# Low rank products on another bank ring, key norms inverted as columns, and a weight load issued later, in the RWKV-7 heads of a hybrid block

## The chip, the cores and the metric

The kernel runs on one core of one Trainium2 chip. The metric is the time of one execution on the device in microseconds (us), lower is better. Everything is float32.

## The reference, cut to what matters

The program is a two layer block (RWKV-7 time mixing, then Hyena, each followed by a mixture of experts). The change lies in the features of the RWKV-7 mixer, which are made for 512 tokens (256 of context, 256 latent) and 16 heads of 64:

```python
wlog = -softplus(-(w0 + tanh(xw @ w1) @ w2)) - 0.5      # one w for each direction z
decay = exp(-exp(wlog))
a = sigmoid(a0 + (xa @ a1) @ a2)                        # one a for each direction z
k = xk @ wrkv[1]
kk = heads(k * k_k)
kk = kk / maximum(norm(kk, axis=-1), 1e-12)
k_dir = k * (1.0 + (a - 1.0) * k_a)
```

After that comes a scan over the tokens in both directions, S = S * w + (S kk) b + v k, with b = kk * a, from which the output rows are read.

## The kernel before, in words

`rwkv_heads` treats two heads (128 channels on the 128 partitions) at a time, in `CH` = 8 groups. The scan is done in chunks of 64 tokens: each group has 8 chain steps (`STEPS`), and each step has three phases, so a round has 24 slots (`SLOTS`). Round m (from -2 to 8) does the chain of group m (`chain`), the matrices of group m + 1 (`now`), and the features of group q = m + 2 (`early`); rows of group m - 1 (`behind`) are finished on the side. Rounds -2 and -1 have no chain yet, rounds 0 to 5 have all of it, round 6 has no `early` part, round 7 has only the chain. Every engine walks the same list of slots in program order: nothing is reordered, so an instruction that waits holds all behind it on its engine.

In each round, TensorE does in phase 0 `chain_state` (products with the state H; VectorE then makes G), in phase 1 `chain_solve` (with G; ScalarE then copies U), in phase 2 `chain_close` (with U; VectorE then makes the new H). Between these stand the other products.

PSUM banks are handed out by two written orders. `OPEN` uses banks 0 and 1 in turn, `INVERSE` banks 2, 3 and 4 in turn; a use may start when the use two (or three) places before it in the order has been read by its reader, ScalarE or VectorE (`BankUses.before`). In `OPEN` the part of slots 14 to 23 reads: wyc(n), h3(m), w0(q), w1(q), k(q), h4(m), a0(q), a1(q), norm(q), h5(m), rg(q). Here h0 to h5 are the six parts of `modulate` (a matrix product with `ada_w` for later layers, summed by VectorE), w and a the low rank products (`low_rank`, L776), k the key projection (`project`, L785), norm the sums of squares, rg the receptance and the gate. So w1 waits until VectorE has read h3 (`modulate(m, 3)`, slot 14, L1493).

The key norms: ScalarE squares k into `kk` (`keys`, L1103) and copies k to `kT` (L1104); TensorE multiplies the 128x512 squares by `head_ones` (L797), which gives each channel the sum of its head; ScalarE takes the root of 128x512 (`norm`, L1107, with a table load); VectorE takes the maximum with 1e-12 (L1298), inverts in two halves of 128x256 (L1301), and multiplies (`unit_keys`, L1305).

The weights of the next group are loaded by SyncE in `load_first` (six transfers, L305 to L310: w2, a2, two blocks of `rw_wrkv` of 512 KB, two parts of g2), in slot 4 of its own list; its semaphore `kr_in` is waited for by the first product of w. SyncE also issues `later.load` (L244, four pieces of `ada_w`) in slots 0, 3, 8, 12, 15 and 19, each after the product before has been done.

Of the kernel before, what the change touches and what calls it, by code (L numbers as in the profile page):

```python
# [17 lines left out]
ALU = mybir.AluOpType  # L18
# [509 lines left out]
def open_order():  # L528

    order = []  # L530
    for m in range(-2, CH + 1):
        chain, now, early, behind = 0 <= m < CH, 0 <= m + 1 < CH, m + 2 < CH, m >= 1
        order += [(m, u) for u in ("bl", "kl") if chain]
        order += [(m, u) for u in ("vl",) if chain]
        order += [(m - 1, u) for u in ("ys",) if behind]
        order += [(m, u) for u in ("h0", "wy0", "wy1") if chain]
        order += [(m, u) for u in ("h1",) if chain]
        order += [(m + 1, u) for u in ("v",) if now]
        order += [(m, u) for u in ("h2",) if chain]
        order += [(m + 1, u) for u in ("bc", "kc", "vc") if now]  # L540
        order += [(m - 1, u) for u in ("rows",) if behind]
        order += [(m + 1, u) for u in ("wyc",) if now]
        order += [(m, u) for u in ("h3",) if chain]
        order += [(m + 2, u) for u in ("w0", "w1", "k") if early]
        order += [(m, u) for u in ("h4",) if chain]
        order += [(m + 2, u) for u in ("a0", "a1") if early]
        order += [(m + 2, u) for u in ("norm",) if early]
        order += [(m, u) for u in ("h5",) if chain]
        order += [(m + 2, u) for u in ("rg",) if early]
    return order  # L550


def inverse_order():

    order = []
    for m in range(-1, CH):
        chain, now = m >= 0, m + 1 < CH
        order += [(m, u) for u in ("z1l", "s1l", "s2l") if chain]
        order += [(m + 1, u) for u in ("pc0", "pc1") if now]
        order += [(m, u) for u in ("z2l",) if chain]  # L560
        order += [(m + 1, u) for u in ("pl00", "pl01", "pl10", "pl11") if now]
        order += [(m, u) for u in ("xl",) if chain]
        order += [(m + 1, u) for u in ("z1c", "s1c", "s2c", "z2c", "xc") if now]
    return order
# [25 lines left out]

OPEN = BankUses(open_order(), 0, 2, lambda name: name == "ys" or name[0] == "h")
INVERSE = BankUses(inverse_order(), 2, 3, lambda name: name[0] in "zp")


def rwkv_heads(s, r, experts, ins, mods):
# [31 lines left out]
    wide = S1b  # L627
    spare = s.take(1)
    later = LaterModulation(s, ins, mods)
# [4 lines left out]
    names = ("ka_ready", "open_done", "open_act", "open_dve", "inv_done", "inv_act", "inv_dve",  # L634
             "sq_ready", "dec_ready", "ex_ready", "bon_ready", "feat_ready", "mask_ready",
             "m_ready", "sel_ready", "turned_in", "base_ready", "spread_ready", "turned_out", "start_ready",
             "h_ready", "g_done", "gs_ready", "u_done", "us_ready", "hy_done", "y_done", "y_ready",
             "y_var", "y_root", "yn_ready", "o_done")
    (ka_ready, open_done, open_act, open_dve, inv_done, inv_act, inv_dve,
     sq_ready, dec_ready, ex_ready, bon_ready, feat_ready, mask_ready,  # L640
     m_ready, sel_ready, turned_in, base_ready, spread_ready, turned_out, start_ready,
# [5 lines left out]
    def rows(n):  # L647
        return slice(n * C, (n + 1) * C)
# [52 lines left out]
    with nc.Block(name="rwkv_heads", no_gpsimd_drain=True) as block:  # L701

        @block.sync
        def _(sp):
            wo_rows = ins["rw_wo"][0].rearrange("(m p) n -> p m n", p=P)

            for m in ROUNDS[:-1]:
# [3 lines left out]
                for slot in range(SLOTS):  # L711
                    if slot == 4 and 0 <= n and n + 1 < CH:
                        sp.wait_ge(open_done, OPEN.done(n, "rg"))
                        r.load_first(sp, ins, n + 1)
# [42 lines left out]
        def _(pe):  # L757
# [12 lines left out]
            def low_rank(n, name):  # L770
                if name == "w":
                    pe.wait_ge(kr_in, 96 * (n + 1))
                w, x = (w2, r.wl) if name == "w" else (a2, r.al)
                banks = [open_bank(n, f"{name}{z}") for z in range(2)]
                for z in range(2):
                    pe.matmul(banks[z][:, :], w[rows(z), :], x[rows(z), :], start=True, stop=True).then_inc(open_done, 1)  # L776

# [17 lines left out]
            def norm(n):  # L795
                pe.wait_ge(sq_ready, n + 1)
                pe.matmul(open_bank(n, "norm")[:, :], s.c("head_ones"), kk, start=True, stop=True).then_inc(open_done, 1)  # L797

# [193 lines left out]
            for m in ROUNDS:  # L992
                n, q = m + 1, m + 2
                chain, now, early, behind = 0 <= m < CH, 0 <= n < CH, q < CH, m >= 1
                for slot in range(SLOTS):
# [37 lines left out]
                    if behind and slot == 13:  # L1033
                        out_rows(m - 1)
                    if now and slot == 14:
                        from_values_early(n)
                    if chain and slot == 14:
                        modulate(m, 3)
                    if early and slot == 14:
                        low_rank(q, "w")  # L1040
                    if early and 15 <= slot < 18:
# [5 lines left out]
                    if early and slot == 18:  # L1047
                        low_rank(q, "a")
                    if early and slot == 19:
                        norm(q)  # L1050
                    if now and slot == 20:
                        level_one(n, 0)
                    if chain and slot == 21:
                        modulate(m, 5)
# [23 lines left out]
        def _(act):  # L1078
# [13 lines left out]
            def decay_rank(n, z):  # L1092
                if n and z == 0:
                    act.wait_ge(feat_ready, n)
                act.activation(sg[z], read(n, f"w{z}")[:, :], ACT.Sigmoid, bias=vec(z, n)).then_inc(open_act, 1)  # L1095

            def rate_rank(n, z):
                bank = read(n, f"a{z}")
                act.activation(steps(BB[n % 2], z), chunks(bank[:, :]), ACT.Sigmoid, bias=vec(2 + z, n)).then_inc(open_act, 1)

# [5 lines left out]
            def norm(n):  # L1106
                act.activation(kk, read(n, "norm")[:, :], ACT.Sqrt).then_inc(open_act, 1)  # L1107

# [93 lines left out]
            for m in ROUNDS:  # L1202
                n, q = m + 1, m + 2
                chain, now, early, behind = 0 <= m < CH, 0 <= n < CH, q < CH, m >= 1
                for slot in range(SLOTS):
# [32 lines left out]
                    if behind and slot == 13:  # L1238
                        act.activation(outT, read(m - 1, "rows")[:, :], ACT.Copy).then_inc(open_act, 1)
                    if now and slot == 14:  # L1240
                        from_values_early(n)
                        spread(n)
                    if early and slot == 14:
                        decay_rank(q, 0)
                        decay_rank(q, 1)
                    if now and slot == 16:
                        place(n, 0)
                    if now and slot == 17:
                        place(n, 1)
                    if early and slot == 18:  # L1250
                        keys(q)
                        rate_rank(q, 0)
                        rate_rank(q, 1)
                    if early and slot == 19:
                        norm(q)
# [13 lines left out]
        def _(dve):  # L1269
            def decay_sum(n, z):  # L1270
                dve.wait_ge(open_act, OPEN.taken(n, f"w{z}")[1])
                for f in range(2):
# [21 lines left out]

            def key_norms(n, f):
                if f == 0:
                    dve.wait_ge(open_act, OPEN.taken(n, "norm")[1])
                    dve.tensor_scalar(kk, kk, 1e-12, None, ALU.max)  # L1298
                    dve.drain()
                c = slice(f * L, (f + 1) * L)  # L1300
                dve.reciprocal(kk[:, c], kk[:, c])  # L1301
                dve.drain()

            def unit_keys(n):
                dve.scalar_tensor_tensor(kk, kT, vec(4, n), kk, ALU.mult, ALU.mult)  # L1305
                dve.drain()

            def key_rates(n):
                dve.wait_ge(open_act, OPEN.taken(n, "a1")[1])
                if n >= 2:  # L1310
# [236 lines left out]
            for m in ROUNDS:  # L1547
                n, q = m + 1, m + 2
                chain, now, early, behind = 0 <= m < CH, 0 <= n < CH, q < CH, m >= 1
                for slot in range(SLOTS):  # L1550
# [37 lines left out]
                    if chain and slot == 11:  # L1588
                        modulate(m, 2)
                    if now and slot == 12:  # L1590
                        base_level(4, wide)
                        bonus(n)
                    if now and slot == 13:
# [31 lines left out]
                    if early and slot == 23:  # L1625
                        unit_keys(q)
                        rates(q)
# [1205 lines left out]
```

## Time and profile before

| what | value |
|---|---|
| median of 3 runs | 1949.21 us (1948.52 to 1949.31) |
| profiled execution, its own time | 1943.13 us |
| its span, first to last instruction | 1941.3 us |
| TensorE matmuls busy | 1727.5 us (89%) |
| VectorE busy | 769.4 us (40%) |
| ScalarE busy | 513.6 us (26%) |
| GpSimd busy | 52.9 us (3%) |
| mean DMA rate | 260 GB/s |

The profiled execution has 1.8 us outside its span. The heads stage lies between about 70 us and 700 us of the span; after it come stages of expert weights. Times in the rows are in us from the start of the span, and an engine's share of busy time is a mean over stages with different limits.

### The profile page before, as it was taken

How to read it: one execution, taken by the hardware profiler on the slowest of the kernel's cores; microseconds unless marked ns; L12 is line 12 of the kernel's file. 1: busy time of each engine (PE TensorE's matmuls, PEld its weight loads, DVE VectorE, ACT ScalarE, POOL GpSimd, SP SyncE). 2: the span in 40 equal slices, each digit the busy share in tenths (PEclk: the TensorE clock that was granted, in tenths of full speed). 3: DMA queues.
4: the chain of work that ended last, by engine and by line, in shares of the span. 5: the costliest groups of instructions: out<-in, count | busy, mean ns of one | idle time of the engine just before them, and what ended most of it. 6: DMA issues, size and time to landing. Idle time of an engine off the chain costs nothing. (4 is left out here: it accounts for less than half of the span.)

```text
span 1941.3 us, 36382 instructions
## 1 busy us (share of the span) xinstructions
PE 1727.5 (89%) x15051; PEld 943.6 (49%) x15051; DVE 769.4 (40%) x1926; ACT 513.6 (26%) x969; POOL 52.9 (3%) x45
## 2 busy tenths in 40 slices
PE   5777887887887888999999999898899999999996
PEld 2345655655655554443443443675654444444442
DVE  5667777776776335210100101565836110110111
ACT  3244454453453121111111111313221111111111
POOL 0001100100100000000000001000000000000001
PEclk8979999998998989999999999999989999999999
DMA  9013323323334477999999997233167999999993
GB/s 311 14 46 100 107 82 117 104 83 110 105 105 137 144 301 311 428 428 429 428 429 428 428 417 278 81 129 124 75 271 300 426 428 429 428 429 429 427 419 123
DMA packets 105463, 504.17 MB, mean 260 GB/s; under 512 B 15840, under 2 KB 60656, under 8 KB 79472
## 3 DMA queue, kind: packets, MB, share of 16 engines
q1 hardware_dynamic: 104064, 501.93, 65.2%
q8 instruction: 99, 1.62, 0.4%
q10 hardware_dynamic: 1264, 0.33, 0.1%
q14 instruction: 36, 0.29, 0.0%
HBM read 501.13 MB, written 1.09 MB: 259 GB/s over the span
## 5 line engine op out<-in xcount | busy, mean ns | idle before, releaser
L2016 DVE TENSOR_TENSOR arena<-banks,arena 128x512 f32<-128x512 f32 x32 | 22.1, 692 | 659.3 <-PE banks L1828 659.3
L1828 PE MATMUL banks<-arena 128*64 128x512 f32 x1024 | 226.2, 594 | 9.5 <-DMA arena<-in_moe_w_up 9.5
L1850 PE MATMUL banks<-arena 128*64 128x512 f32 x1024 | 226.8, 595 | 3.3 <-ACT arena L1947 3.3
L1819 PE MATMUL banks<-arena 128*64 128x512 f32 x1024 | 225.3, 592 | 3.3 <-DVE arena L1939 3.3
L785 PE MATMUL banks<-arena 128*128 128x512 f32 (+1 forms) x384 | 166.0, 571 | 3.2 <-ACT arena L1095 3.0
L1828 PEld LDWEIGHTS banks<-arena 128*64 128x64 f32 x1024 | 81.4, 137 | 152.3 <-issue 152.2
L1819 PEld LDWEIGHTS banks<-arena 128*64 128x64 f32 x1024 | 74.3, 137 | 147.8 <-issue 144.2
L1850 PEld LDWEIGHTS banks<-arena 128*64 128x64 f32 x1024 | 70.7, 137 | 154.5 <-issue 150.7
L1941 ACT ACTIVATE arena<-banks,arena 128x128 f32<-128x128 f32 x128 | 48.2, 457 | 334.1 <-PE banks L1808 334.1
L1808 PEld LDWEIGHTS banks<-arena 128*128 128x128 f32 x1024 | 118.3, 194 | 28.1 <-issue 24.3
L1808 PE MATMUL banks<-arena 128*128 128x128 f32 x1024 | 124.4, 280 | 3.5 <-DVE arena L2011 3.5
L1857 PE MATMUL banks<-arena 128*128 128x512 f32 x256 | 115.4, 593 | 2.4 <-ACT arena L1952 2.4
L785 PEld LDWEIGHTS banks<-arena 128*128 128x128 f32 x384 | 72.1, 201 | 60.8 <-issue 46.8
L1951 ACT ACTIVATE arena<-banks 128x512 f32<-128x512 f32 x32 | 19.1, 597 | 282.5 <-PE banks L1850 282.5
L2435 PE MATMUL banks<-arena 128*128 128x256 f32 x384 | 87.5, 386 | 0.0
L1939 DVE TENSOR_SCALAR arena<-banks,arena 128x128 f32<-128x128 f32 x128 | 43.7, 404 | 96.9 <-PE banks L1808 96.9
L2435 PEld LDWEIGHTS banks<-arena 128*128 128x128 f32 x384 | 73.4, 193 | 16.7 <-issue 6.6
L1857 PEld LDWEIGHTS banks<-arena 128*128 128x128 f32 x256 | 46.1, 190 | 50.0 <-issue 45.9
L1932 ACT ACTIVATE arena<-banks 128x512 f32<-128x512 f32 x32 | 19.1, 597 | 169.7 <-PE banks L1819 169.7
L253 PE MATMUL banks<-arena 128*32 128x96 f32 (+1 forms) x1536 | 48.1, 265 | 9.0 <-DMA arena<-in_ada_w 5.3
L776 PE MATMUL banks<-arena 64*128 64x512 f32 x64 | 22.2, 768 | 28.6 <-DVE arena L1493 20.3
L1475 DVE SCALAR_TENSOR_TENSOR arena<-banks,arena 128x64 f32<-128x64 f32 x112 | 26.8, 280 | 50.5 <-PE banks L967 47.3
(401 smaller groups left out, 2433.3 us busy)
## 6 DMA issues: line engine op xcount, KB each, us to landing
arena<-in_moe_w_gate SPq DMA_DIRECT2D x64, 2048.0 KB, 14.9
arena<-in_moe_w_up SPq DMA_DIRECT2D x64, 2048.0 KB, 17.1
arena<-in_moe_w_down SPq DMA_DIRECT2D x64, 2048.0 KB, 13.3
arena<-in_ada_w SPq DMA_DIRECT2D x128, 192.0 KB, 2.9
arena<-in_ada_w SPq DMA_DIRECT2D x64, 256.0 KB, 3.6
arena<-in_rw_wrkv SPq DMA_DIRECT2D x24, 512.0 KB, 5.1
arena<-in_hy_w_in SPq DMA_DIRECT2D x6, 2048.0 KB, 8.6
arena<-in_ada_w SPq DMA_DIRECT2D x8, 1024.0 KB, 16.8
```

What stands on the lines that cost most here:

```text
L253: mm = pe.matmul(bank[g * 32:(g + 1) * 32, 0:n], self.cond[:, half * self.HALF + t], self.w[t][:, g * n:(g + 1) * n], start=(t == 0), stop ...
L776: pe.matmul(banks[z][:, :], w[rows(z), :], x[rows(z), :], start=True, stop=True).then_inc(open_done, 1)
L785: mm = pe.matmul(s.psum[OPEN.bank(n, name)][:, 0:width], wkv[k][:, t], x[:, t], start=(t == 0), stop=(t == KT - 1))
L1475: dve.scalar_tensor_tensor(H[:, z], s.psum[5 + z][:, 2 * C:3 * C], fade[m % 2][:, z, j:j + 1], Hf[:, z], ALU.mult, ALU.add)
L1808: mm = pe.matmul((X0, X1)[k // 4][:, k % 4 * P:(k % 4 + 1) * P], hx[:, t, k * P:(k + 1) * P], sel[par][:, t].rearrange("p a b -> p (a b)") ...
L1819: mm = pe.matmul(G[j * CAP:(j + 1) * CAP, :], xT[:, t, j * CAP:(j + 1) * CAP], wg[par][j][:, t], start=(t == 0), stop=(t == KT - 1))
L1828: mm = pe.matmul(U[j * CAP:(j + 1) * CAP, :], xT[:, t, j * CAP:(j + 1) * CAP], wu[j][:, t], start=(t == 0), stop=(t == KT - 1))
L1850: mm = pe.matmul(bank[j * CAP:(j + 1) * CAP, :], hT[:, t, j * CAP:(j + 1) * CAP], wd[j][:, t, half * 512:(half + 1) * 512], start=(t == 0) ...
L1857: pe.matmul(OUT[k][:, :], selwT[par][:, k // 2], y[:, k % 2 * 512:(k % 2 + 1) * 512], start=start, stop=stop).then_inc(scat_done, 1)
L1939: op = eng.tensor_scalar(xT[:, k], src, sc[:, k:k + 1], sh[:, k:k + 1], ALU.mult, ALU.add)
L1941: op = eng.activation(xT[:, k], src, ACT.Identity, bias=sh[:, k:k + 1], scale=sc[:, k:k + 1])
L2435: mm = pe.matmul(s.psum[n % 2][:, 0:L], win_ring[k][:, t, q * P:(q + 1) * P], hT[:, t], start=(t == 0), stop=(t == KT - 1))
```

## The change

There are four edits.

1. The low rank products w0, w1, a0, a1 leave `OPEN` and take banks of `INVERSE`, between xl(m) and z1c(m + 1). TensorE issues w in slot 13 instead of 14 and a in slot 14 instead of 18; ScalarE reads w in slot 13 instead of 14, and a in slot 17 instead of 18.
2. The key norms are made as 128x8: TensorE uses a block of 128 tokens of the squares as the stationary operand and two columns of `head_ones` as the moving one, four times, so the sums stand with tokens on the partitions. ScalarE takes the root of 128x8, VectorE the maximum and the inverse of 128x8, and TensorE spreads them back to 128x512 with eight products of a broadcast column with the identity (`spread_norms`, a new use "inv" of `OPEN`, slot 20), which VectorE reads from PSUM in `unit_keys` (slot 21 instead of 23). TensorE's norm moves from slot 19 to 18. A root of one element at the end of slot 17 draws the table load ahead.
3. `load_first` is issued in slot 9 instead of 4.
4. On VectorE `modulate(m, 0)` moves from slot 3 to 2 and `bonus` from slot 12 to 11.

```diff
@@ open_order
-        order += [(m + 2, u) for u in ("w0", "w1", "k") if early]
+        order += [(m + 2, u) for u in ("k",) if early]
         order += [(m, u) for u in ("h4",) if chain]
-        order += [(m + 2, u) for u in ("a0", "a1") if early]
-        order += [(m + 2, u) for u in ("norm",) if early]
+        order += [(m + 2, u) for u in ("norm", "inv") if early]
@@ inverse_order
-    for m in range(-1, CH):
-        chain, now = m >= 0, m + 1 < CH
+    for m in range(-2, CH):
+        chain, now, early = m >= 0, 0 <= m + 1 < CH, m + 2 < CH
...
         order += [(m, u) for u in ("xl",) if chain]
+        order += [(m + 2, u) for u in ("w0", "w1", "a0", "a1") if early]
         order += [(m + 1, u) for u in ("z1c", "s1c", "s2c", "z2c", "xc") if now]
@@ SyncE
-                    if slot == 4 and 0 <= n and n + 1 < CH:
+                    if slot == 9 and 0 <= n and n + 1 < CH:
                         sp.wait_ge(open_done, OPEN.done(n, "rg"))
                         r.load_first(sp, ins, n + 1)
@@ TensorE
-                banks = [open_bank(n, f"{name}{z}") for z in range(2)]
+                banks = [inverse_bank(n, f"{name}{z}") for z in range(2)]
...
             def norm(n):
                 pe.wait_ge(sq_ready, n + 1)
-                pe.matmul(open_bank(n, "norm")[:, :], s.c("head_ones"), kk, start=True, stop=True).then_inc(open_done, 1)
+                bank = open_bank(n, "norm")
+                for t in range(TOK // P):
+                    mm = pe.matmul(bank[:, 2 * t:2 * t + 2], kk[:, t * P:(t + 1) * P], s.c("head_ones")[:, 0:P:HEAD], start=True, stop=True)
+                mm.then_inc(open_done, 1)
+
+            def spread_norms(n):
+                bank = open_bank(n, "inv")
+                pe.wait_ge(inv_norms, n + 1)
+                for t in range(TOK // P):
+                    for h in range(2):
+                        one = norms[:, 2 * t + h:2 * t + h + 1].to_broadcast([P, HEAD])
+                        mm = pe.matmul(bank[rows(h), t * P:(t + 1) * P], one, s.c("ident"), start=True, stop=True)
+                mm.then_inc(open_done, 1)
...
+                    if early and slot == 13:
+                        low_rank(q, "w")
...
                     if early and slot == 14:
-                        low_rank(q, "w")
+                        low_rank(q, "a")
...
                     if early and slot == 18:
-                        low_rank(q, "a")
-                    if early and slot == 19:
                         norm(q)
...
+                    if early and slot == 20:
+                        spread_norms(q)
@@ ScalarE
-                act.activation(kk, read(n, "norm")[:, :], ACT.Sqrt).then_inc(open_act, 1)
+                act.activation(norms, read(n, "norm")[:, 0:2 * TOK // P], ACT.Sqrt).then_inc(open_act, 1)
...
+                    if early and slot == 13:
+                        decay_rank(q, 0)
+                        decay_rank(q, 1)
...
+                    if early and slot == 17:
+                        rate_rank(q, 0)
+                        rate_rank(q, 1)
+                        act.activation(spare, s.c("ones")[:, 0:1], ACT.Sqrt)
                     if early and slot == 18:
                         keys(q)
-                        rate_rank(q, 0)
-                        rate_rank(q, 1)
-                    if early and slot == 19:
                         norm(q)
@@ VectorE
-                c = slice(f * L, (f + 1) * L)
-                dve.reciprocal(kk[:, c], kk[:, c])
-                dve.drain()
+            def key_norms(n):
+                dve.wait_ge(open_act, OPEN.taken(n, "norm")[1])
+                dve.tensor_scalar(norms, norms, 1e-12, None, ALU.max)
+                dve.drain()
+                dve.reciprocal(norms, norms).then_inc(inv_norms, 1)
             def unit_keys(n):
-                dve.scalar_tensor_tensor(kk, kT, vec(4, n), kk, ALU.mult, ALU.mult)
+                dve.wait_ge(open_done, OPEN.done(n, "inv"))
+                bank = s.psum[OPEN.bank(n, "inv")]
+                dve.scalar_tensor_tensor(kk, kT, vec(4, n), bank[:, :], ALU.mult, ALU.mult).then_inc(open_dve, 1)
...
+                    if chain and slot == 2:
+                        modulate(m, 0)
                     if chain and slot == 3:
                         level_z(m, "z1l", Z1)
-                        modulate(m, 0)
...
+                    if now and slot == 11:
+                        bonus(n)
...
                     if early and slot == 19:
+                        key_norms(q)
                         decay_centre(q, 1)
                     if early and slot == 20:
-                        key_norms(q, 0)
                         key_rates(q)
                     if early and slot == 21:
-                        key_norms(q, 1)
+                        unit_keys(q)
```

## Rows read from the trace of the kernel before

**Rows 1.** Busy time by engine in stretches; after it the TensorE clock and DMA share

```profile
364.00:434.00 70.00, 58.53 (x1182) 40.04 (x1181) 52.29 (x133) 34.78 (x64) 5.02 (x4) 0.98 0.35 103
...
402.70:406.10 3.40, 3.27 (x22) 1.34 (x19) 1.40 (x4) 1.42 (x3) 0.00 (x0) 0.50 0.31 80
```

**Rows 2.** TensorE's waits, 150 to 640 us: us in total, times, longest

```profile
PE banks L776 <- DVE arena L1493: 20.3, 6, 3.6
PE banks L884 <- DVE arena L1496: 11.3, 7, 1.6
...
PE banks L841 <- issue: 6.6, 4, 3.8
...
PE banks L894 <- issue: 5.0, 3, 3.2
```

**Rows 3.** Timeline of TensorE, round 3, slots 3 and 5

```profile
371.42 1.15 PE L884 MATMUL banks<-arena 64*64 64x64 f32 x32 [1.61 <-DVE arena L1496]
...
374.65 1.16 PE L841 MATMUL banks<-arena 64*64 64x64 f32 x64 [0.69 <-ACT x_res L1156]
```

**Rows 4.** Timeline of TensorE, round 3, slots 14 to 22

```profile
402.29 1.71 PE L776 MATMUL banks<-arena 64*128 64x512 f32 x4 [3.35 <-DVE arena L1493]
...
404.77 2.64 PE L785 MATMUL banks<-arena 128*128 128x512 f32 x4
...
407.83 2.84 PE L785 MATMUL banks<-arena 128*128 128x512 f32 x6
...
416.62 1.13 PE L776 MATMUL banks<-arena 64*128 64x512 f32 x4 [0.54 <-DVE arena L1496]
...
418.58 1.10 PE L797 MATMUL banks<-arena,const 128*128 128x512 f32 x2 [0.34 <-ACT arena L1099]
...
424.89 0.27 PE L953 MATMUL banks<-arena 64*64 64x64 f32 x2 [1.25 <-DVE arena L1462]
```

**Rows 5.** Timeline of VectorE, round 3, slots 14 and 20

```profile
400.84 0.48 DVE L1475 SCALAR_TENSOR_TENSOR arena<-banks,arena 128x64 f32<-128x64 f32 x2 [0.18 <-issue]
...
401.89 0.26 DVE L1493 TENSOR_TENSOR arena<-banks,arena 128x96 f32<-128x96 f32 x1 [0.16 <-issue]
...
421.63 1.75 DVE L1301 RECIPROCAL arena<-arena 128x256 f32<-128x256 f32 x1
```

**Rows 6.** Timeline of ScalarE, round 3, slots 16 to 19

```profile
408.00 5.39 ACT L1194 ACTIVATE arena<-x_res,const 128x256 f32<-128x256 f32 x8
...
417.75 1.26 ACT L1099 ACTIVATE arena<-banks,arena 128x512 f32<-128x512 f32 x2 [2.58 <-PE banks L776]
...
419.20 1.28 ACT L1107 ACT_TABLE_LOAD   x1
```

**Rows 7.** Timeline of TensorE, round 6, slot 5

```profile
594.05 1.24 PE L841 MATMUL banks<-arena 64*64 64x64 f32 x36 [3.84 <-issue]
```

**Rows 8.** Timeline of SyncE's queue: load_first in round 3, and a load of round 6

```profile
371.07 0.43 SPq L305 DMA_DIRECT2D arena<-in_rw_w  x1
...
375.12 0.43 SPq L310 DMA_DIRECT2D arena<-in_rw_g  x1
...
585.11 0.43 SPq L726 DMA_DIRECT2D arena<-in_rw_wo  x1
```

**Rows 9.** DMA issues, 360 to 434 us: KB each, median us to landing

```profile
arena<-in_rw_wrkv SPq DMA_DIRECT2D x3, 512.0 KB, 4.8
```

**Rows 10.** Timeline of TensorE, round 4, slots 0 and 1

```profile
433.06 0.35 PE L953 MATMUL banks<-arena 64*64 64x64 f32 x5 [0.68 <-DVE arena L1460]
...
434.14 0.44 PE L816 MATMUL banks<-arena,const 128*64 128x128 f32 x4
...
434.84 0.39 PE L818 MATMUL banks<-arena,const 128*64 128x128 f32 x4
```

**Rows 11.** Timeline of VectorE, round -2

```profile
89.48 0.43 DVE L1298 TENSOR_SCALAR arena<-arena 128x512 f32<-128x512 f32 x1 [8.13 <-ACT arena L1107]
```

**Rows 12.** Timeline of TensorE, first product of round -1

```profile
103.19 1.99 PE L841 MATMUL banks<-arena 64*64 64x64 f32 x64 [10.48 <-DVEq L1356]
```

More of the change, by code:

```diff
@@ L588, in before @@
         return (self.kind[i], self.nth[i]) if i >= 0 else (None, 0)
-OPEN = BankUses(open_order(), 0, 2, lambda name: name == "ys" or name[0] == "h")
+OPEN = BankUses(open_order(), 0, 2, lambda name: name in ("ys", "inv") or name[0] == "h")
 INVERSE = BankUses(inverse_order(), 2, 3, lambda name: name[0] in "zp")
@@ L627, in rwkv_heads @@
     wide = S1b
-    spare = s.take(1)
+    spare, norms = s.take(1), s.take(2 * TOK // P)
     later = LaterModulation(s, ins, mods)
@@ L634, in rwkv_heads @@
     names = ("ka_ready", "open_done", "open_act", "open_dve", "inv_done", "inv_act", "inv_dve",
-             "sq_ready", "dec_ready", "ex_ready", "bon_ready", "feat_ready", "mask_ready",
+             "sq_ready", "inv_norms", "dec_ready", "ex_ready", "bon_ready", "feat_ready", "mask_ready",
              "m_ready", "sel_ready", "turned_in", "base_ready", "spread_ready", "turned_out", "start_ready",
@@ L639, in rwkv_heads @@
     (ka_ready, open_done, open_act, open_dve, inv_done, inv_act, inv_dve,
-     sq_ready, dec_ready, ex_ready, bon_ready, feat_ready, mask_ready,
+     sq_ready, inv_norms, dec_ready, ex_ready, bon_ready, feat_ready, mask_ready,
      m_ready, sel_ready, turned_in, base_ready, spread_ready, turned_out, start_ready,
@@ L773, in low_rank @@
                 w, x = (w2, r.wl) if name == "w" else (a2, r.al)
-                banks = [open_bank(n, f"{name}{z}") for z in range(2)]
+                banks = [inverse_bank(n, f"{name}{z}") for z in range(2)]
                 for z in range(2):
-                    pe.matmul(banks[z][:, :], w[rows(z), :], x[rows(z), :], start=True, stop=True).then_inc(open_done, 1)
+                    pe.matmul(banks[z][:, :], w[rows(z), :], x[rows(z), :], start=True, stop=True).then_inc(inv_done, 1)
             def project(n, name, tiles):
@@ L1094, in decay_rank @@
                     act.wait_ge(feat_ready, n)
-                act.activation(sg[z], read(n, f"w{z}")[:, :], ACT.Sigmoid, bias=vec(z, n)).then_inc(open_act, 1)
+                act.activation(sg[z], read_inverse(n, f"w{z}")[:, :], ACT.Sigmoid, bias=vec(z, n)).then_inc(inv_act, 1)
             def rate_rank(n, z):
-                bank = read(n, f"a{z}")
-                act.activation(steps(BB[n % 2], z), chunks(bank[:, :]), ACT.Sigmoid, bias=vec(2 + z, n)).then_inc(open_act, 1)
+                bank = read_inverse(n, f"a{z}")
+                act.activation(steps(BB[n % 2], z), chunks(bank[:, :]), ACT.Sigmoid, bias=vec(2 + z, n)).then_inc(inv_act, 1)
             def keys(n):
@@ L1242, in _ @@
                         spread(n)
-                    if early and slot == 14:
-                        decay_rank(q, 0)
-                        decay_rank(q, 1)
                     if now and slot == 16:
@@ L1270, in decay_sum @@
             def decay_sum(n, z):
-                dve.wait_ge(open_act, OPEN.taken(n, f"w{z}")[1])
+                dve.wait_ge(inv_act, INVERSE.taken(n, f"w{z}")[1])
                 for f in range(2):
@@ L1293, in decay_centre @@
                 dve.tensor_tensor(sg[z], cum[z], sg[z], ALU.subtract).then_inc(dec_ready, 1)
[L1295 to L1298, printed above, removed]
-                    dve.drain()
-                c = slice(f * L, (f + 1) * L)
-                dve.reciprocal(kk[:, c], kk[:, c])
+            def key_norms(n):
+                dve.wait_ge(open_act, OPEN.taken(n, "norm")[1])
+                dve.tensor_scalar(norms, norms, 1e-12, None, ALU.max)
                 dve.drain()
+                dve.reciprocal(norms, norms).then_inc(inv_norms, 1)
             def unit_keys(n):
-                dve.scalar_tensor_tensor(kk, kT, vec(4, n), kk, ALU.mult, ALU.mult)
+                dve.wait_ge(open_done, OPEN.done(n, "inv"))
+                bank = s.psum[OPEN.bank(n, "inv")]
+                dve.scalar_tensor_tensor(kk, kT, vec(4, n), bank[:, :], ALU.mult, ALU.mult).then_inc(open_dve, 1)
                 dve.drain()
             def key_rates(n):
-                dve.wait_ge(open_act, OPEN.taken(n, "a1")[1])
+                dve.wait_ge(inv_act, INVERSE.taken(n, "a1")[1])
                 if n >= 2:
@@ L1589, in _ @@
                         modulate(m, 2)
+                    if now and slot == 11:
+                        bonus(n)
                     if now and slot == 12:
                         base_level(4, wide)
-                        bonus(n)
                     if now and slot == 13:
@@ L1625, in _ @@
                     if early and slot == 23:
-                        unit_keys(q)
                         rates(q)
```

## The prediction

> **What bounds the kernel now.** I first read busy time by stretches, because the 89% of TensorE is a mean over stages, and only the heads stage (about 70 to 700 us) is touched; what follows it begins when the last chain step is done, so a saving there should pass to the end one for one. In round 3, 364 to 434 us, TensorE is busy for 58.5 of 70 us and VectorE for 52.3 [rows 1]: neither is full, and both run in a written order, so the round is long where one stands and waits for the other. Next come TensorE's waits. The largest, 20.3 us in six rounds, is the first low rank product waiting for VectorE's L1493, and the next, 11.3 us, is L884 waiting for L1496; behind them stand waits put down to "issue", which means that nothing in the program held the instruction [rows 2]. The timeline then shows what each stands in front of. In slot 14 TensorE is ready 3.35 us before 402.29, and the only thing it lacks is a bank of `OPEN` [rows 4]: VectorE has made H by 401.3 and reads h3 at 401.89 [rows 5]. The chain's next product stands behind those low rank products, so the whole chain waits. The clock falls with the idle stretch: it is at 0.50 (1.2 GHz) from 402.7 to 406.1 [rows 1], and four passes of L785 take 2.64 us where six take 2.84 later [rows 4].
>
> **Edit 1, the low rank products.** In `INVERSE` the banks of w0 and w1 are those of pl10 and pl11, long read by VectorE in slot 8; a0 has that of xl, read in slot 8 too, and a1 that of w0. So w (1.13 us at full clock, four passes [rows 4]) and a (the same) go into the hole of 3.35 us, which is larger than both. The chain product then goes when H is there, at about 401.4 instead of 403.9: 2.5 us. With the hole the half clock should go: the four passes at 2.84 / 6 = 0.47 us each are 1.9 for 2.64, 0.7 us. Lead by slot 16: 3.2 us. Then a is no longer in slot 18: its 1.13 and the wait of 0.54 before it [rows 4] come off, lead 4.8 us. Cover for w on ScalarE: it sits in front of the copy of wyc, some 2 us before `spread` is wanted, and costs nothing; without that cover it would cost its own 1.3 us.
>
> **Edit 2, the norms.** ScalarE does the placing, 5.39 us in one piece from 408.00 [rows 6]. It starts 3.2 us earlier, at about 404.9, and ends at 410.3; then the new order has a's two sigmoids (1.26), the table load (1.28) [rows 6] and the root of one element (0.2, taken as the floor of a small instruction), then the square (0.7) and the copy of k (0.5 more). The norm needs the copy, since its bank is k's. That is 414.3, and TensorE is there at 412.95: a new wait of 1.35 us, lead 3.45. The old wait of 0.34 before L797 goes, +0.35. The four new products have no row of their own: between nothing and the 1.10 us of the old one [rows 4]; I take them as equal. Between the chain's slots 19 and 20 nothing stands any more to hide ScalarE's copy of U: -0.4. `spread_norms` is 16 passes of half width against 128 columns; L816 and L818 with 16 passes run from 434.14 to 435.23 [rows 10], so 1.1 us: -1.1, lead 2.3. The inverse of 128x8 and the maximum are at most two times the 0.43 us that the 512 wide maximum takes [rows 11], and at least nothing; I take 0.5 for both. VectorE so loses 0.43 + 1.75 + 1.75 us [rows 5, 11] and gains 0.5: 3.4 us a round. What is late next: the first receptance product has the bank of "inv", which VectorE frees only in `unit_keys` in slot 21, behind the decay centring, the new H, the key rates and G. By the durations these have now, that is at about 421.1, when TensorE has been ready for 1.5 us (bounds: nothing, and 3 if the centring starts late). That wait takes -1.5, but the one of 1.25 us before L953 [rows 4], which stood behind a long inverse, goes, and so does the 0.68 us before the first L953 of the next round [rows 10], as `unit_keys` is no longer at the end. Lead at the end: 2.3 - 1.5 + 1.25 + 0.68 = 2.75 us for each of the six full rounds.
>
> The table load is where a rule of the skill speaks against this change. The trace has 1.28 us and the next activation directly behind it, at 420.49 against 419.20 + 1.28 [rows 6]. The Trainium skill, "ScalarE: Activation LUTs", section "What ACT_TABLE_LOAD costs", adds a drain of 1.38 us to every switch; by that the square would come so much later and a round would lose as much again. The trace does not agree for the load itself.
>
> **Edit 4.** L884 in slot 3 waits 1.61 us for h0 to be read [rows 3]. Read in slot 2, it is free when TensorE comes. The next wait, 0.69 us for S1 [rows 3], moves too, but then the features on VectorE bind, which end only some 0.5 us earlier plus 0.2 for the moved sum; I keep 1.4 of 1.61 us. Bonus in slot 11 lies in VectorE's dense part either way: nothing.
>
> **Edit 3, the load.** SyncE issues its six transfers from 371.07 to 375.5 [rows 8]; 512 KB take 4.8 us to land [rows 9]. In the stretch after them TensorE runs hundreds of short products and stands for "issue" 6.6 + 5.0 us in all [rows 2]. I read these as instruction blocks that come late behind the big transfers; the 3.84 us at 594.05 in round 6, where `load_first` does not run but the output weights are loaded from 585.11, speaks for that [rows 7, 8]. So 11.6 - 3.8 = 7.8 us are this load's. In slot 9 it flows beside the value projection, with few, long passes. I take 7 us in all (bounds: nothing, and 12 with the half clock that follows such holes). The Trainium skill, "Runtime: NRT & Kernel Launch", section "Instruction fetch mechanics", calls the crossing into a new block "mostly hidden"; by it the move would be worth nothing. The waits of 3 us here do not agree. Other side: w is wanted in slot 13, some 17 us after slot 8 begins. Behind `later.load` the six issues end about 7.5 us into that, landing takes 5 to 6: 4 us are to spare.
>
> **The rounds without all parts.** In round -2 all is one line of dependences up to L841 at 103.19, which waited 10.48 us for features [rows 12]. VectorE's 3.4 us and ScalarE's 512 wide roots come out, a no longer stands between k and its norm, and the receptance comes up to 1 us later: 5 us. Round -1 has the same, but ScalarE's placing holds the square back and "inv" the receptance: 1 us. Rounds 6 and 7 have only edit 4: 2.4 us.
>
> **Sum.** 6 x (2.75 + 1.4) = 24.9; load 7; rounds -2 and -1 6; rounds 6 and 7 2.4: 40.3 us. Against the profiled execution's own 1943.1 (its span is 1941.3) that is 1903. The median of the runs is 6.1 us above that execution, so I put the median after at 1949.2 - 40.3 = 1909 us.
>
> **Rivals.** (a) The load's move is worth nothing, since blocks come late wherever a big load runs: 40.3 - 7 = 33, 1916 us. For it: small gaps exist elsewhere too. Against: slots 9 to 12 show no issue wait now. Chance 0.15.
>
> (b) The norm's new round trip becomes the bound: ScalarE's square, TensorE, the root, VectorE, TensorE, VectorE, each with a semaphore, ahead of a bank that TensorE needs. If the two new waits are twice what I took (2.7 and 3.0), the full rounds give 4.15 - 2.85 = 1.3, in all 23 us: 1926 us. For it: two engines with strict order in the loop. Chance 0.17. With the page's drain it would be in between: 6 x 1.4 = 8 us less than mine, 1917.
>
> (c) More than forecast: VectorE's 3.4 us count in full at the end of the round and the half clock goes everywhere: 50 us and more, under 1899 us. Chance 0.1.
>
> (d) Slower: the six transfers come late for w. The wait of w now stands in slot 13, in front of `chain_close`, so all engines stop with it. With 4 us to spare and 33 us to lose, each of six rounds must wait 5.5 us, so the last transfer would have to land 9.5 us later than by its row, three times as long. Price at 12 us late: 6 x 8 = 48, so 1957 us. Chance 0.03.
>
> (e) No change, as the slots' gains are eaten by the next wait of VectorE: 1949 us. Against: the hole in slot 14 is in every full round. Chance 0.03.
>
> **How the numbers follow.** My forecast (34 to 50 us less) has 0.52. Its own range is 1899 to 1916. The range for 8 in 10 leaves out (c)'s far half, (d), (e) and the worst of (b): 1894 to 1929 us. No change means within 0.2%, or 4 us, about what a measurement of this kernel can tell. Faster: forecast, (a), (b), (c), 0.94; same 0.03; slower 0.03.
>
> **What would show it.** L776 in slot 13 and no wait before it; no half clock at slot 14; VectorE's time down by some 27 us in eight rounds; a wait of 1 to 2 us before the norm's products, released by ScalarE's L1104, and one before the receptance, released by `unit_keys`; L884 without its 1.61 us; no issue waits in slots 5 to 7 of rounds 0 to 5. I am wrong if w waits for a DMA, if issue waits show up in slots 9 to 14 instead, or if the wait for "inv" is 3 us or more.

## The result and the profile after

The changed kernel has a median of 1896.84 us (4 runs) beside 1949.26 us: 0.9729 of the time before, 95% interval 0.9694 to 0.9764, so 46 to 60 us less. A later run of the same kernel on another occasion gave 0.9775 (0.9750 to 0.9801), 39 to 49 us less; the two intervals overlap between 46 and 49 us. The forecast was 40.3 us. The first median lies 2 us below the forecast's own range of 1899 to 1916 us and inside its wider range of 1894 to 1929 us. The span of the profiled execution fell from 1941.3 to 1897.9 us, 43.4 us, and all but 0.3 of it is there when ScalarE starts the last copy of U of the heads stage (689.63 us before, 646.55 after). Behind it nothing is gained or lost.

First the page's busy times (share of the span, instructions), then one full round, round 3, with the two stretches around its norm: after the duration stand busy times of TensorE, its weight loads, VectorE, ScalarE and GpSimd, then the TensorE clock and the DMA share. The round takes 65.2 us for 70.

```profile
PE 1735.3 (91%) x15227; PEld 961.4 (51%) x15227; DVE 746.2 (39%) x1918; ACT 511.1 (27%) x977; POOL 56.2 (3%) x45
```

```profile
344.70:409.90 65.20, 58.87 (x1186) 41.79 (x1185) 48.85 (x130) 34.16 (x66) 5.48 (x4) 0.97 0.37 111
379.00:393.70 14.70, 12.59 (x156) 6.78 (x152) 11.10 (x29) 11.42 (x19) 0.00 (x0) 1.00 0.24 74
393.70:397.10 3.40, 3.24 (x94) 3.03 (x95) 2.49 (x10) 0.46 (x2) 0.00 (x0) 0.50 0.43 156
```

TensorE does as much work in the round as before (58.9 for 58.5 us, [rows 1]) and stands less. VectorE works 3.4 us less in this round, as forecast; over the whole kernel it is 23.2 us less (746.2 for 769.4), where 27 were forecast. The half clock has not gone, it has moved: behind slot 14 the clock is full, and 0.50, which is 1.2 GHz, stands in 393.7 to 397.1, right behind the norm. Each of the six full rounds has such a stretch of 3.4 us, which begins 0.8 to 1.8 us after the norm's first product. TensorE's waits, 150 to 610 us (us in total, times, longest), show why:

```profile
PE banks L799 <- ACT arena L1118: 8.7, 6, 1.7
PE banks L865 <- DVE arena L1393: 5.9, 7, 0.8
PE banks L946 <- DVEq L1490: 5.3, 8, 2.0
PE banks L853 <- DVEq L1370: 5.1, 6, 1.0
PE banks L785 <- DVE arena L1319: 4.5, 6, 0.8
```

The 20.3 and 11.3 us of [rows 2] are gone. In their place stands the norm (L799), which waits for ScalarE's copy of k, and the receptance (L785), which waits for `unit_keys` (L1319). TensorE's timeline of round 3 gives both places, and the low rank products (L776) without a wait, to be read against [rows 4]:

```profile
375.26 1.13 PE L776 MATMUL banks<-arena 64*128 64x512 f32 x4
...
378.56 1.13 PE L776 MATMUL banks<-arena 64*128 64x512 f32 x4
380.11 0.34 PE L946 MATMUL banks<-arena 64*64 64x64 f32 x8 [0.42 <-DVEq L1490]
...
380.50 1.98 PE L785 MATMUL banks<-arena 128*128 128x512 f32 x4
...
392.84 1.09 PE L799 MATMUL banks<-const,arena 128*128 128x2 f32 x8 [1.69 <-ACT arena L1118]
...
397.32 1.09 PE L808 MATMUL banks<-const,arena 128*64 128x128 f32 x16
...
400.36 1.56 PE L785 MATMUL banks<-arena 128*128 128x256 f32 x6 [0.76 <-DVE arena L1319]
```

The first four key passes take 1.98 us for 2.64, as forecast for the full clock. The four norm products take 1.09 us though they write 128x2 each: the profile counts eight passes for them (x8), and they take no less than the two passes of the one 128x512 product did (1.10). ScalarE and VectorE at the same place:

```profile
390.14 1.28 ACT L1267 ACT_TABLE_LOAD   x1
391.43 0.20 ACT L1267 ACTIVATE arena<-const 128x1 f32<-128x1 f32 x1
391.54 0.67 ACT L1117 ACTIVATE arena<-banks,arena 128x512 f32<-128x512 f32 x1
392.11 0.59 ACT L1118 ACTIVATE arena<-banks 128x512 f32<-128x512 f32 x1
```

```profile
394.18 0.17 DVE L1312 TENSOR_SCALAR arena<-arena 128x8 f32<-128x8 f32 x1 [2.33 <-ACT arena L1121]
394.43 0.20 DVE L1314 RECIPROCAL arena<-arena 128x8 f32<-128x8 f32 x1
```

The drawn table load costs 1.28 us and the next activation follows it at once: the drain that the Trainium skill ("ScalarE: Activation LUTs", "What ACT_TABLE_LOAD costs") adds to every switch is not there. And VectorE stands 2.33 us for the root with its decay centring, which needs no root, queued behind. The experiments begin with that question: does edit 2 gain anything?

### The profile page after: what moved, and what is told of

Same layout as the page of the kernel before. It is cut to its first block and busy times, and to the rows that moved or that the text cites. A ratio compares the mean times of both kernels' runs of the same rounds, so it can differ in the third digit from the quotient of the medians.

```text
span 1897.9 us, 36726 instructions
## 1 busy us (share of the span) xinstructions
PE 1735.3 (91%) x15227; PEld 961.4 (51%) x15227; DVE 746.2 (39%) x1918; ACT 511.1 (27%) x977; POOL 56.2 (3%) x45
## 3 DMA queue, kind: packets, MB, share of 16 engines
HBM read 501.13 MB, written 1.09 MB: 265 GB/s over the span
## 5 line engine op out<-in xcount | busy, mean ns | idle before, releaser
L785 PE MATMUL banks<-arena 128*128 128x512 f32 (+1 forms) x384 | 159.1, 552 | 4.5 <-DVE arena L1319 4.5
L785 PEld LDWEIGHTS banks<-arena 128*128 128x128 f32 x384 | 70.5, 197 | 57.5 <-issue 44.3
L253 PE MATMUL banks<-arena 128*32 128x96 f32 (+1 forms) x1536 | 48.2, 266 | 6.6 <-DMA arena<-in_ada_w 5.6
L2220 POOL TENSOR_TENSOR x_res<-x_res,arena 128x512 f32<-128x512 f32 x8 | 9.9, 1266 | 1280.2 <-DVEq L2196 1280.2
L253 PEld LDWEIGHTS banks<-arena 128*32 128x32 f32 x1536 | 35.9, 112 | 15.7 <-issue 12.9
## 6 DMA issues: line engine op xcount, KB each, us to landing
arena<-in_moe_w_gate SPq DMA_DIRECT2D x64, 2048.0 KB, 14.9
```

What stands on the lines that cost most here:

```text
L253: mm = pe.matmul(bank[g * 32:(g + 1) * 32, 0:n], self.cond[:, half * self.HALF + t], self.w[t][:, g * n:(g + 1) * n], start=(t == 0), stop ...
L785: mm = pe.matmul(s.psum[OPEN.bank(n, name)][:, 0:width], wkv[k][:, t], x[:, t], start=(t == 0), stop=(t == KT - 1))
```

## The experiments

In each set of runs the kernel before was run beside the others; its medians were 1946.24 us (the four single edits), 1945.87 us (the order, the version that beats both, edits 1 and 2) and 1947.53 us (the rest). The ratio is to these runs, with its 95% interval in brackets. "us less" is that ratio applied to the median before, so it can differ by up to 2.5 us from the difference of the two medians.

**Each edit alone**, on the kernel before (the hunks are those of the diff above, one edit at a time).

> The kernel before with edit 1 alone (low rank products in the level ring, w in slot 13, a in slot 14). My theory of the prediction: 3.2 us a full round by slot 16 and 1.67 more by slot 18, all kept but a little at the norm: some 27 us less over six full rounds, 1922 us, no wait of L776 for VectorE and no half clock around slot 14. Rival (the wait only moves to the next thing that VectorE is late with, the long inverses in slots 20 and 21): only the slot 16 lead survives, 19 us or less, 1930 us, and the wait of L953 for L1462 grows above its 8 us.

Measured: 1915.16 us, 0.9849 (0.9817 to 0.9881), 29.4 us less. The wait of the low rank products for VectorE is gone, no half clock stands around slot 14, and the rival's wait does not grow: the one for the sum behind the long inverse fell from 8.1 to 0.7 us. What came instead is a transfer: `modulate` now comes sooner than its weights, since `later.load` may be issued only when the product before is done. TensorE's waits, 150 to 640 us:

```profile
PE banks L253 <- DMA arena<-in_ada_w: 16.8, 9, 2.9
PE banks L884 <- DVE arena L1497: 12.9, 8, 1.6
```

> The kernel before with edit 2 alone (norms as 128x8, spread by TensorE), low rank products where they were. My theory: the spread costs 1.1 us a round and the two waits behind the long inverses (1.25 and 0.68 us) go, so under 1 us a round, and 4 us in round -2: 5 to 9 us less, 1940 to 1944 us. Rival (VectorE's 3.4 us a round count in full): 20 us or more less, under 1930 us. Second rival (the wait for the bank of the spread eats it): no change or slower, 1949 us or more.

Measured: 1958.25 us, 1.0049 (1.0027 to 1.0071), 9.5 us **slower**. My number was wrong, and the second rival was right in sign and in kind: TensorE's receptance now waits for the bank of the spread, 9.6 us in the six full rounds (TensorE's waits, 150 to 650 us):

```profile
PE banks L785 <- DVE arena L1318: 9.6, 6, 1.6
```

The cause on VectorE stands in its timeline in slot 19 of one round:

```profile
434.41 0.17 DVE L1311 TENSOR_SCALAR arena<-arena 128x8 f32<-128x8 f32 x1 [4.24 <-ACT arena L1121]
434.65 0.20 DVE L1313 RECIPROCAL arena<-arena 128x8 f32<-128x8 f32 x1
```

The inverse costs 0.20 us where two took 3.5, but VectorE stands 4.24 us in front of it (25.4 us in six rounds). What the edit saves in work it loses in standing, and the spread comes on top.

> The kernel before with edit 3 alone (load_first in slot 9 instead of 4). My theory: issue waits of slots 5 to 7 in rounds 0 to 5 go, 7 us less, 1942 us. Rival (instruction blocks come late wherever the load runs, or the waits have another cause): within 3 us of 1949, with issue waits of the same sum elsewhere.

Measured: 1938.78 us, 0.9957 (0.9941 to 0.9973), 8.4 us less. TensorE's issue waits from 150 to 570 us, that is rounds 0 to 5, before:

```profile
PE banks L894 <- issue: 4.3, 2, 3.2
PE banks L253 <- issue: 3.7, 2, 3.0
PE banks L841 <- issue: 2.8, 3, 1.5
PE banks L859 <- issue: 0.4, 1, 0.4
```

and with the load in slot 9:

```profile
PE banks L253 <- issue: 1.5, 2, 0.7
PE banks L841 <- issue: 0.9, 2, 0.7
```

11.2 us became 2.4. The difference, 8.8 us, is about the gain, and none appears in slots 9 to 12. The spans of these two profiled executions differ by only 2.0 us (1941.3 and 1939.3); the second has 44 us at half clock in rounds 0 to 5 for 31. The time rests on the twelve runs.

> The kernel before with edit 4 alone (modulate(m, 0) in slot 2, bonus in slot 11). My theory: 1.4 us of the 1.61 us before L884 are kept in each of eight rounds: 11 us less, 1938 us. Rival (the features on VectorE bind in slots 3 to 5, so the wait moves to L841): 0.6 us a round, 5 us less, 1944 us, with L841 waiting for VectorE instead.

Measured: 1933.99 us, 0.9925 (0.9905 to 0.9946), 14.6 us less (10.5 to 18.5). My theory's 11 lies in the interval, the rival's 5 does not. TensorE's wait of L884 for L1496, 11.3 us before [rows 2], is gone, but the rival's sign is there too: L841 now waits for VectorE, 5.7 us in all (150 to 640 us), where it waited 4.8 us for ScalarE before.

```profile
PE banks L841 <- DVEq L1356: 5.7, 6, 1.0
```

The spans of the two profiled executions differ by only 6.8 us (1941.3 and 1934.5); the time rests on the six runs, not on that pair.

**Edit 2 further.** First VectorE's order in slot 19, on edit 2 alone and on the whole change:

```diff
                     if early and slot == 19:
-                        key_norms(q)
                         decay_centre(q, 1)
+                        key_norms(q)
```

> Edit 2 alone with decay_centre(q, 1) ahead of key_norms(q). Theory A: VectorE's idle 4.2 us before the maximum in slot 19 is filled, and with it edit 2 alone is no longer slower: about 12 us less than edit 2 alone (ratio to before about 0.998). Theory B (spread's passes and the wait for its bank cost it in any order): still slower than before by some 0.4%.

Measured: 1946.29 us, 0.9990 (0.9967 to 1.0012). Theory A held: the order was worth 0.6%, and edit 2 alone then does no harm, nor any good. VectorE's wait for the root fell from 25.4 to 14.1 us in six rounds; it was shortened, not filled.

> The changed kernel with decay_centre(q, 1) ahead of key_norms(q) in slot 19 of VectorE. Theory A (edit 2 costs time because VectorE stands for the root in slot 19 with the decay centring behind it, 2.3 us a round in the changed kernel): the centring fills that idle time, the wait of 0.76 us for the bank of the spread goes, 5 to 8 us less than the changed kernel's 1897. Theory B (the cost is TensorE's own 16 more passes and the half clock after the norm's wait): no change, 1897 us, the waits as before.

Measured: 1899.88 us, 0.9751 (0.9719 to 0.9784): no change that can be told from the changed kernel. Theory A failed here. VectorE's wait for the root falls (0.83 us in the same round), but the wait for the bank of the spread stays, 4.2 us in six rounds. It does not stand behind the centring: `unit_keys` (L1319) follows the sum G (L1476), which follows a product of TensorE's that comes only behind the spread. VectorE's timeline:

```profile
391.08 0.17 DVE L1312 TENSOR_SCALAR arena<-arena 128x8 f32<-128x8 f32 x1 [0.83 <-ACT arena L1121]
...
396.99 0.42 DVE L1476 TENSOR_TENSOR arena<-banks,arena 128x256 f32<-128x256 f32 x1 [2.67 <-PE banks L950]
...
397.68 0.75 DVE L1319 SCALAR_TENSOR_TENSOR arena<-arena,banks 128x512 f32<-128x512 f32 x1
```

The next two ask what edit 2 adds in company: edits 1 and 2 together, and the whole change without edit 2.

> Edits 1 and 2 without 3 and 4. With edit 1 the a products and sigmoids are out of the norm's way, so the round trip starts earlier than VectorE's other work ends. Theory A: edit 2 on top of edit 1 saves 2 to 8 us where alone it lost 9.5, ratio to before 0.981 to 0.984. Rival: it loses its 9.5 here too, ratio 0.990, and the gap between the sum of the four single edits (42.9 us) and the whole change (52.8 us) comes from edits 3 and 4 together.

Measured: 1924.64 us, 0.9875 (0.9841 to 0.9910). Edit 1 alone had 0.9849, in another set of runs: edit 2 shows no saving on top of it. My theory's range is missed; the loss is between nothing and the rival's.

> Edits 1, 3 and 4, norms as before. The three alone gave 29.4 + 8.4 + 14.6 = 52.4 us. Theory A: they add up, and edit 2 gives nothing inside the whole change: ratio to before 0.971 to 0.976, as the changed kernel. Rival: the single gains overlap, and edit 2 makes up 10 us of the whole change: ratio 0.978 or above.

> The changed kernel unaltered, beside the three others on the same chip: 0.971 to 0.976 of the time before. It is the yardstick for the differences of a few us.

Measured side by side: without edit 2 1897.07 us, 0.9750 (0.9726 to 0.9775); the changed kernel 1902.50 us, 0.9775 (0.9750 to 0.9801), just above what was expected. The three edits add up, and edit 2 inside the change is worth nothing or costs some 5 us: the two intervals just overlap. TensorE's waits without edit 2, 150 to 610 us, show why taking out the norm's wait brings so little:

```profile
PE banks L253 <- DMA arena<-in_ada_w: 14.9, 9, 2.6
```

In the changed kernel this line has 4.0 us in the same stretch. Without the norm's wait TensorE comes to `modulate` (L253) sooner and stands there for the weights instead, and in five of the six full rounds a stretch at half clock follows that wait, just as it follows the norm's.

> The changed kernel with load_first back in slot 4. Theory A (the load's cost is instruction blocks that come late): issue waits back in slots 5 to 8 of rounds 0 to 5, some 5 to 9 us slower than the changed kernel, ratio to before 0.976 to 0.978. Rival (block borders have moved with the new instruction count, so no such waits): same as the changed kernel.

Measured: 1914.83 us, 0.9838 (0.9814 to 0.9863), 12.3 us slower than the changed kernel beside it, more than I expected. Between 150 and 570 us (rounds 0 to 5 and the first slots of round 6) the issue waits are 14.9 us for 11.0 in the changed kernel beside it. The largest in round 3, in TensorE's timeline:

```profile
361.08 0.33 PE L971 MATMUL banks<-arena 64*64 64x64 f32 x5 [2.25 <-issue]
```

These 3.9 us are a third of it. The stretches at half clock between 150 and 570 us sum to 34 us for 24, and 10 us more at half clock can cost up to 5. The rest is open.

What an issue wait stands for can be read from the transfers. The profile has a queue of its own for instructions, q8, with transfers of 16 KB. TensorE's longest such wait in rounds 0 to 5 of the kernel before, in round 4, and that queue between 445.8 and 447.1 us:

```profile
448.58 0.69 PE L894 MATMUL banks<-x_res,arena 64*64 64x64 f32 x8 [3.16 <-issue]
```

```profile
q8 instruction: 1, 0.02, 5.8%
```

The transfer lands at 447.1, and TensorE goes on 1.5 us later. All eight issue waits of 0.3 us or more in rounds 0 to 5 of the kernel before end 1.2 to 1.5 us after such a landing, and so do those of the same stretch in the changed kernel beside it and with the load back in slot 4 (1.3 to 1.7 us). So they are waits for instructions. The transfers themselves are not slow: 0.9 to 1.8 us each, 1.1 in the middle, in the kernel before. What makes one start late no run shows.

**A version that beats both.** ScalarE's second placing moves behind the root; what it writes is needed only in slot 2 of the next round. Once with edit 2 and the new order of VectorE, once without edit 2:

```diff
-                    if now and slot == 17:
-                        place(n, 1)
...
                         norm(q)
+                    if now and slot == 19:
+                        place(n, 1)
```

> As the last one, and ScalarE's place(n, 1) moved from slot 17 to 19, behind the root. The wait before the norm's products (8.7 us in six rounds) stands behind 5.39 us of placing; half of it moved, the square comes 2.7 us earlier. If that wait is on the path: 1.5 us a round, and the half clock stretch after it goes too, 0.7 to 1.5 us a round: 13 to 18 us less than with the order alone, near 1877 us. If the path runs over VectorE or the chain there: under 4 us less.

Measured: 1879.30 us, 0.9645 (0.9612 to 0.9679), 69 us less than before, and 20.6 less than the order alone, more than the 13 to 18 expected; 5.9 of it lies ahead of round 0, which the expectation had left out. TensorE's norm comes without a wait, and no stretch at half clock is left in rounds 0 to 5. Timeline, and stretches as above:

```profile
377.54 0.87 PE L253 MATMUL banks<-arena 128*32 128x96 f32 x32
378.33 1.05 PE L799 MATMUL banks<-const,arena 128*128 128x2 f32 x8
```

```profile
364.00:378.00 14.00, 13.65 (x210) 7.64 (x209) 12.19 (x29) 10.48 (x18) 0.00 (x0) 1.00 0.28 88
378.00:382.00 4.00, 3.74 (x132) 3.37 (x126) 3.47 (x14) 2.37 (x6) 0.00 (x0) 1.00 0.54 156
```

> Edits 1, 3 and 4, norms as before, and ScalarE's place(n, 1) in slot 19 behind the root. Theory A: the placing hurts only by the norm's new early place in slot 18 and its clock stretch, so here it gives under 5 us, and edit 2 pays only together with it. Rival: the placing is what counts, and this is as fast as the version with both (ratio 0.9645), so that edit 2 is worth nothing in any company.

Measured: 1890.55 us, 0.9713 (0.9689 to 0.9737), 6.5 us less than without the move (1897.07), where I had allowed 5. The interval does not touch that of the version with edit 2 (up to 0.9679). So the version with edit 2 is about 0.7% ahead, once the placing is out of the norm's way. That comparison is over two occasions, and this version has the new order besides; on the changed kernel the order alone gave nothing. Where the difference lies, TensorE's waits from 150 to 640 us show, with edit 2 and without:

```profile
PE banks L253 <- DMA arena<-in_ada_w: 9.5, 8, 3.4
```

```profile
PE banks L253 <- DMA arena<-in_ada_w: 18.1, 12, 3.5
```

Without edit 2 TensorE stands twice as long for the weights of `modulate`, and rounds 0 to 5 have 13.7 us at half clock, where the version with edit 2 has none. A rival is therefore untested: edit 2's extra passes may gain only by giving that transfer time. No run issues the transfer sooner.

## Why the prediction was right, and where it was not

**Edit 1** (28.8 us by the forecast, 4.8 a round until slot 18): shown. Alone it gives 29.4 us. The hole went and the passes run at full clock. Not foreseen: where TensorE comes sooner, the weights of `modulate` come late (16.8 us of waits with edit 1 alone, 17.9 with edits 1, 3 and 4); in the whole change, where the norm's wait comes first, it is 5.6 us (all 150 to 640 us).

**Edit 2.** The forecast had it as a loss in the full rounds, from 4.8 to 2.75 us of lead, 12.3 us in six, set against 6 us in the first two rounds. In company it measured a loss of 5.4 us (1902.50 against 1897.07, with intervals that overlap). That this is near the forecast's sum, a loss of 6.3, is partly luck: in the profiles the full rounds lose 6.2 us by edit 2 and not 12.3, and the first two rounds lose too and do not gain. The wait before the norm was forecast at 1.35 us and measured 1.45 on average (8.7 / 6). The wait for the bank of the spread was forecast at 1.5 and is 0.75 (4.5 / 6). The sign that failed is the half clock: at slot 14 it went, as forecast, but behind the new wait it comes back in each full round. I had looked at holes that the change fills and not at those it makes. It is not edit 2's alone: without edit 2 it comes back in five of six rounds, behind the wait for the weights of `modulate`. My expectation for edit 2 alone failed at another step: I counted the inverses as gone and did not see that VectorE's list puts the wait for the root ahead of the centring, which had covered it before.

**Rounds -2 and -1** (6 us forecast): too much, and not by the edit that was credited. The first chain step's copy of U is at 152.20 after and 154.16 before; the stage itself began 0.9 us later, so 2.9 us. Counted in the same way, edit 1 alone gives 4.7 us here, edit 2 alone under half a us, and edits 1, 3 and 4 without edit 2 give 4.9: inside the change edit 2 costs 2 us. In round -1 TensorE stands for ScalarE, which is at its placing:

```profile
137.13 1.40 PE L799 MATMUL banks<-const,arena 128*128 128x2 f32 x8 [3.79 <-ACT arena L1117]
```

I had named this cause and priced it too low. With the placing moved, the same two rounds are 5.9 us shorter.

**Edit 3** (7 us): the effect is shown, by the run alone: 8.8 us of issue waits and 8.4 us of time. The forecast had counted 7.8 us of such waits in rounds 0 to 5; with the 3.7 us of L253, which it left out, they were 11.2. That TensorE stands there for instructions is shown by the landings above; that the big load is what delays them is argued. It is not the whole cause: in the changed kernel the load runs in slot 9, and yet 7.8 us of issue waits are left between 150 and 570 us (11.0 in the later run's profile), all in slots 4 to 8. The sign "no issue waits in slots 5 to 7" was so nearly met with edit 3 alone (2.4 us left) and failed in the whole change. Undoing the edit in the changed kernel costs 12.3 us, so the term was small, but only 3.9 of these are issue waits. The Trainium skill, "Runtime: NRT & Kernel Launch", section "Instruction fetch mechanics", calls the crossing into a new block "mostly hidden". The trace of the kernel before agrees for most: of the 54 transfers of that queue between 150 and 570 us, eight were followed by a wait of 0.3 us or more. Those eight are what the edit is about.

**Edit 4** (1.4 us a round in six rounds, and the 2.4 us of rounds 6 and 7: 10.8 us): 14.6 us alone (10.5 to 18.5), so the forecast is at the lower edge of what was measured.

**The sum.** 29.4 - 9.5 + 8.4 + 14.6 = 42.9 us from the single edits, and 43.8 and 52.8 us for all in the two measurements. In the profiles the full rounds gave 34.9 us where 31.9 were forecast, and rounds 6 and 7 gave 6.2 us where 2.4 were forecast; round 6 holds the issue wait of 3.84 us of [rows 7], whose counterpart after is 1.48. Since the change has shifted the instructions against the block borders, part of that may be chance. The total was met with terms that erred both ways: edit 4, the load in company and rounds 6 and 7 gave more, the first two rounds less. The mechanism of the largest term, edit 1, was right; the nearness of the total is in part luck. The rivals: (a), the load's move worth nothing, is refuted as to time. (b), the round trip as the bound, was right in kind: it ate all that edit 2 could give, but its two waits were not twice what the sum had (1.45 and 0.75 us, not 2.7 and 3.0). (c), more than forecast, came closest to the first measurement, but its reasons did not hold: the half clock did not go everywhere, and edit 2, which makes VectorE cheaper, gave nothing. (d), w waiting for its weights, is refuted: no product waits for them.

## What to carry to other kernels

Where every engine walks a fixed list, making an operation cheaper gives nothing if the engine must then stand for its input: look at what is queued behind the wait, and whether it covered that wait before. A long operation on the way of a new, short round trip (here the second half of 5.4 us of placing, which nobody needed yet) is worth moving before the round trip is judged. When one wait goes, look for the next in the same place: here the wait for the weights of `modulate` stood behind the norm's. A hole can cost twice, because a stretch at half clock can follow it: the norm's wait, 1.4 to 1.7 us in every full round, was followed by one in all six rounds of the changed kernel's profile, in five in the profile of its later run, and in four with the new order of VectorE, where the waits were the same.

## What the runs showed of the hardware that was not expected

Two products of VectorE (128x512, both operands and result in SBUF) take 1.29 us together when GpSimd is idle and 3.00 us when they meet GpSimd's mask products. The same line of VectorE in round -2 of the changed kernel, where GpSimd has nothing to do, and in round 3:

```profile
91.81 1.29 DVE L1337 TENSOR_TENSOR arena<-arena 128x512 f32<-128x512 f32 x2
```

```profile
403.69 3.00 DVE L1337 TENSOR_TENSOR arena<-arena 128x512 f32<-128x512 f32 x2
```

GpSimd at the second place:

```profile
403.19 1.28 POOL L747 TENSOR_TENSOR arena<-arena,const 128x512 f32<-128x512 f32 x1 [43.96 <-PE banks L906]
404.42 1.72 POOL L748 TENSOR_TENSOR arena<-arena,const 128x512 f32<-128x512 f32 x1
```

GpSimd's second product takes 1.72 us for 1.28. In the six full rounds of the kernel before only the first of the two met GpSimd, and the pair took 2.20 us, so `key_products` is 0.8 us longer in each of them after the change. These 4.8 us are about what VectorE's total saving, 23.2 us, falls short of the 27 forecast. It is a matter of when they run and not of edit 2 alone: with edits 1, 3 and 4 the pair takes over 3 us in five full rounds too. What the meeting costs in the time of the kernel no run shows.
